# One core, two-layer trunk: the first V tiles take the last four U tiles from SBUF, gates are stored in pieces, one row of U per tile

## The chip, the core and the metric

The kernel runs on one core of one Trainium2 chip. The metric is the device time of one execution in microseconds. The median of three runs of the kernel before is 3313.8 us (3308.7 to 3314.72).

## The reference

Two layers. Layer 0 mixes with mLSTM heads and a short convolution, layer 1 with stick-breaking attention. After each mixer stands the same PEER block, which the change touches: every token picks 8 x 16 = 128 of 16384 experts by product keys, and each expert is one row of `expert_u` and one of `expert_v`.

```python
def peer_ffn(h, w_query, sub_keys1, sub_keys2, expert_u, expert_v):
    ...                                   # q, s1, s2, two top-k, softmax
    expert = e1 * PEER_NKEYS + e2
    def block(args):
        xt, et, gt = args
        act = jax.nn.gelu(jnp.einsum("td,thkd->thk", xt, expert_u[et]), approximate=False) * gt
        return jnp.einsum("thk,thkd->td", act, expert_v[et])
```

## The kernel before

All activations are float32; each matmul operand is split in a high and a low part, and three matmuls make one product. Weights come as a stream of 613 tiles of 128 x 1024 (`raw`, 512 KB, a ring of four, loaded by SyncE). ScalarE makes `w_hi` (L497), and `w_lo` is made by GpSimd (L434) or by VectorE (L1667).

The PEER block of a layer computes 384 of the 512 tokens densely, over all 16384 experts, and the last 128 tokens by fetching each token's own 128 rows of U and V ("fetched" tokens, one row of every token at a time, 512 KB).

The dense part is 128 U tiles (one per second key, numbered n), then 128 V tiles (numbered v). A U tile is 24 matmuls of 384 columns (L924 to L926), after which ScalarE takes gelu into `gel`, a ring of four slots (L679), and stores 192 KB of it to DRAM (`gel_dram`, L681). A V tile is 18 matmuls of 512 columns (L944), which sum the product of gelu and gate with V.

The gates come up during U tiles 27 to 116: VectorE builds one-hot planes for four tokens at a time (a quad, L1676 and L1680), TensorE multiplies them (L1176), and ScalarE and VectorE collect the result in `stage`. Twelve quads are a batch of 48 tokens; there are eight. ScalarE stores a batch of 3072 KB to `g_dram` in one DMA (L722); the eighth goes out at tile n = 117. The stage has 48 x 4 bytes x 128 keys = 24 KB in a row per partition.

At n = 121 (`FIRST_UNIT_AT`) ScalarE waits until all gates and the first eight gelus are in DRAM and loads two units. A unit is what four V tiles need: `gates` (768 KB, L730) and `gin`, the gelus (768 KB, L732). VectorE multiplies them (`product`, L1724), ScalarE rounds (`a_hi`, L740), VectorE subtracts (`a_lo`, L1732). This runs V_AHEAD = 5 tiles ahead of TensorE, so its first five stand in U tiles 123 to 127; unit 2 is loaded at n = 127. ScalarE loads the next unit when VectorE has finished the one before the last.

In each U tile from 27 on GpSimd fetches one row of U (L451) and VectorE takes its dot product with the token (`dot`, L1699); behind tile 117 there are two rows per tile. The ring `u_rows` has three slots. The rows left over, 17 of 128, follow one per V tile. GpSimd fetches rows of V (L459) once the last U tile is done, since their buffer lies over `h_lo`, and VectorE adds them up (L1711, L1714).

In U tiles up to 116 GpSimd makes `w_lo`; from 117 on VectorE does, two tiles ahead (`LOW_AHEAD`). Every engine's order is written out by hand. In a U tile ScalarE does `w_hi` of tile n + 3, the quads' copies, gelu, the store, and then what the tile number adds. In a V tile VectorE does `w_lo` of v + 2, `product` of v + 5, a dot if one is left, the row of V, and `a_lo` of v + 5. In layer 0 one of seven V tiles also has a dot product for the modulation (`ada_w`, 512 KB).

## Time and profile before

| | us |
|---|---|
| median of three runs | 3313.8 |
| profiled execution, device time | 3312.34 |
| its span | 3310.6 |
| TensorE busy | 3108.2 |
| VectorE busy | 2745.8 |

| transfer | KB each | count |
|---|---|---|
| raw (weight tile) | 512 | 613 |
| gel_dram store | 192 | 256 |
| g_dram store | 3072 | 16 |
| gates load, gin load | 768 | 64 each |

Of 317118 DMA packets all but 2366 are under 8 KB; the sixteen stores of gates have 128 rows of 24 KB each, 2048 in all. The profile's page gives busy time by engine, then the span in 40 slices, the queues, the chain that ended last, and the costliest groups. The timeline lists single instructions; in brackets stands how long the engine was idle ahead of one and what ended that.

### The profile page before, as it was taken

To read this page: it belongs to the slowest core of one execution; us is meant where nothing else is said; L and a number is where in the kernel's file an instruction comes from. 1 tells how busy PE (TensorE), PEld (TensorE's weight loads), DVE (VectorE), ACT (ScalarE), POOL (GpSimd) and SP (SyncE) were. 2 spreads that over 40 slices of the span, in tenths; PEclk is the share of its full clock that TensorE was granted. 3 is DMA by queue.
4 is the path that set the end of the run, shared out by engine and by line. 5 is a ranking of instruction groups with operands and counts; after the bars stand their busy time and mean duration, and the time that the engine had idled before them with its cause. 6 is when DMAs were issued, how large, how long until landed. Compare 5 with 4: busy or idle time off the path is not lost.

```text
span 3310.6 us, 44003 instructions
## 1 busy us (share of the span) xinstructions
PE 3108.2 (94%) x15340; PEld 2686.9 (81%) x15340; DVE 2745.8 (83%) x4632; ACT 1290.8 (39%) x1910; POOL 1532.8 (46%) x880
## 2 busy tenths in 40 slices
PE   4898999999997899999899998999999988999999
PEld 3776799999996677887777667899999976788887
DVE  6677898999996788887776658998999977878887
ACT  3233334444442233333344763344444432333332
POOL 3333346666664434344333003456666654556221
PEclk9899999999998999999999999999999998999999
DMA  5633246898889999999624013258898999999996
GB/s 220 204 121 110 75 129 202 291 319 300 311 307 339 369 367 354 359 367 354 249 77 153 1 51 118 96 174 271 305 317 308 314 325 359 366 366 358 366 354 234
DMA packets 317118, 849.16 MB, mean 256 GB/s; under 512 B 26144, under 2 KB 157232, under 8 KB 314752
## 3 DMA queue, kind: packets, MB, share of 16 engines
q1 hardware_dynamic: 90448, 329.82, 28.4%
q0 software_dynamic: 74000, 268.81, 22.6%
q10 hardware_dynamic: 152480, 248.02, 20.7%
q8 instruction: 117, 1.92, 0.2%
q14 instruction: 73, 0.60, 0.1%
HBM read 743.78 MB, written 102.76 MB: 256 GB/s over the span
## 4 chain that ended last, share of the span: by engine, by line
PE 45%; DVE 28%; DMA 14%; issue 8%; POOL 3%; ACT 1%; ACTq 0%; POOLq 0%; DVEq 0%; SPq 0%
PE banks L944 14%; DVE u_rows L1699 9%; PE gbank L944 7%; DVE plane L1680 6%; DMA u_rows<-u_dram,row_of 6%; DVE hot L1676 6%; DMA gin<-gel_dram 3%; PE banks L904 3%; PE banks L906 3%; PE banks L905 3%; DVE stage L1690 3%; DMA ada_w<-ada_dram 2%; PE banks L924 2%; PE banks L926 2%; PE banks L925 2%
## 5 line engine op out<-in xcount | busy, mean ns | idle before, releaser
L434 POOL TENSOR_TENSOR w_lo<-raw,w_hi 128x1024 fp32r<-128x1024 f32 x339 | 829.2, 2448 | 775.3 <-ACT w_hi L497 771.2
L497 ACT ACTIVATE w_hi<-raw 128x1024 fp32r<-128x1024 f32 x613 | 647.6, 1057 | 494.2 <-PE banks L944 229.2
L924 PE MATMUL banks<-h_hi,w_hi 128*128 128x384 f32 x2048 | 690.5, 337 | 31.2 <-DVE w_lo L1667 17.0
L925 PE MATMUL banks<-h_lo,w_hi 128*128 128x384 f32 x2048 | 688.3, 336 | 0.0
L926 PE MATMUL banks<-h_hi,w_lo 128*128 128x384 f32 x2048 | 688.0, 336 | 0.0
L459 POOL DMA_INDIRECT v_rows<-v_dram,row_of x256 | 421.6, 1647 | 532.0 <-DVE fetched L1714 518.4
L451 POOL DMA_INDIRECT u_rows<-u_dram,row_of x256 | 273.8, 1069 | 440.3 <-DVE z L1699 434.1
L1699 DVE CUSTOM_DVE_ANT_0 u_rows<-u_rows,h_rows 128x1024 f32<-128x1024 f32 x256 | 410.7, 1605 | 65.2 <-DMA u_rows<-u_dram,row_of 64.8
L924 PEld LDWEIGHTS banks<-h_hi,w_hi 128*128 128x128 f32 x2048 | 387.3, 189 | 33.0 <-DVE w_lo L1667 18.3
L925 PEld LDWEIGHTS banks<-h_lo,w_hi 128*128 128x128 f32 x2048 | 387.4, 189 | 0.0
L926 PEld LDWEIGHTS banks<-h_hi,w_lo 128*128 128x128 f32 x2048 | 387.0, 189 | 0.0
L1714 DVE SCALAR_TENSOR_TENSOR fetched<-v_rows,share,fetched 128x1024 f32<-128x1024 f32 x254 | 324.9, 1279 | 19.0 <-DMA v_rows<-v_dram,row_of 18.3
L1667 DVE TENSOR_TENSOR w_lo<-raw,w_hi 128x1024 fp32r<-128x1024 f32 x274 | 333.9, 1219 | 4.7 <-ACT w_hi L497 4.7
L740 ACT ACTIVATE a_hi<-gin 128x384 fp32r<-128x384 f32 x256 | 133.6, 522 | 490.9 <-DVE gin L1724 482.8
L944 PE MATMUL banks<-w_hi,a_hi 128*128 128x512 f32 x1024 | 321.9, 396 | 0.0
L944 PE MATMUL banks<-w_hi,a_lo 128*128 128x512 f32 x1024 | 319.8, 394 | 0.0
L944 PE MATMUL banks<-w_lo,a_hi 128*128 128x512 f32 x1024 | 318.8, 393 | 0.0
L904 PE MATMUL banks<-h_hi,w_hi 128*128 128x512 f32 x696 | 285.5, 410 | 2.2 <-DVE h_lo L1832 1.4
L906 PE MATMUL banks<-h_hi,w_lo 128*128 128x512 f32 x696 | 272.8, 392 | 0.0
L905 PE MATMUL banks<-h_lo,w_hi 128*128 128x512 f32 x696 | 272.5, 392 | 0.0
L679 ACT ACTIVATE gel<-banks 128x384 f32<-128x384 f32 x256 | 125.7, 491 | 356.1 <-PE banks L926 341.3
L1680 DVE TENSOR_TENSOR plane<-hot,banks 128x1024 fp32r<-128x1024 f32 x192 | 234.4, 1221 | 6.6
(316 smaller groups left out, 4852.2 us busy)
## 6 DMA issues: line engine op xcount, KB each, us to landing
raw<-stream_dram SPq DMA_DIRECT2D x613, 512.0 KB
gel_dram<-gel ACTq DMA_DIRECT2D x256, 192.0 KB
g_dram<-stage ACTq DMA_DIRECT2D x16, 3072.0 KB
gates<-g_dram ACTq DMA_DIRECT2D x64, 768.0 KB
gin<-gel_dram ACTq DMA_DIRECT2D x64, 768.0 KB
ada_w<-ada_dram ACTq DMA_DIRECT2D x50, 512.0 KB, 4.8
ada_out<-ada_dram ACTq DMA_DIRECT2D x18, 512.0 KB, 4.7
ada_first<-ada_dram SPq DMA_DIRECT2D x8, 1024.0 KB, 20.0
```

What stands on the lines that cost most here:

```text
L434: pool.tensor_tensor(w_lo[:, s, :], raw[:, s, :], w_hi[:, s, :].bitcast(F32), ALU.subtract).then_inc(split_lo, 1)
L459: pool.indirect_dma_start(v_rows[:, j % V_ROWS, :], None, (v0, v1)[layer], bass.IndirectOffsetOnAxis(ap=row_of[:, j:j + 1], axis=0)).then_ ...
L497: act.activation(w_hi[:, s, :], raw[:, s, :], ACT.Copy).then_inc(split_hi, 1)
L904: pe.matmul(out, wh, hi(k), start=(k == 0), stop=False)
L905: pe.matmul(out, wh, lo(k), start=False, stop=False)
L906: mm = pe.matmul(out, wl, hi(k), start=False, stop=(k == DC - 1))
L924: pe.matmul(out, wh, h_hi[:, k, 0:DENSE_T], start=(k == 0), stop=False)
L925: pe.matmul(out, wh, h_lo[:, k, 0:DENSE_T], start=False, stop=False)
L926: mm = pe.matmul(out, wl, h_hi[:, k, 0:DENSE_T], start=False, stop=(k == DC - 1))
L944: mm = pe.matmul(sums[c][half][:], a, w[:, half * SEQ:(half + 1) * SEQ], start=(v == 0 and a is ah and w is hi), stop=(v == NKEYS - 1 and ...
L1680: dve.tensor_tensor(plane[:, q % 2].rearrange("p t n e -> p n t e"), hot[:, q % 2, 1].bitcast(F32).unsqueeze(1).to_broadcast(full), parts[ ...
L1699: dve.tensor_tensor_reduce(row, row, h_rows[:], 1.0, 0.0, ALU.mult, ALU.add, z[:, j:j + 1]).then_inc(S("dotted"), 1)
```

## The change

- Unit 0 of V is now the last four U tiles. V on the host is rolled by four tiles, so V tile 0 is key 124. The gelus of n = 124 to 127 are not stored and not loaded: `product`, `a_hi` and `a_lo` of V tiles 0 to 3 work on `gel`. Unit 0 loads only gates.
- `V_AHEAD` is 3: the first three products stand in U tiles 125 to 127, the fourth in V tile 0. Unit 2 is loaded in V tile 1.
- A batch of gates is stored as four pieces of 32 keys (768 KB, rows of 6 KB), one per U tile for the first seven batches. The four pieces of the eighth batch all go at n = 117.
- One row of U per tile up to n = 127, so 101 rows in U tiles and 27 in V tiles (111 and 17 before). `u_rows` has four slots.

```diff
--- before.py
+++ after.py
@@ -24,7 +24,9 @@
 PH = 8
 TOPK = 16
 NKEYS = 128
-V_AHEAD = 5
+V_AHEAD = 3
+
+KEPT = 4
 A_RING = 8
 UNIT = 4
 
@@ -36,11 +38,12 @@
 DENSE_T = SEQ - FETCHED
 DENSE_C = DENSE_T // P
 PICKS = PH * TOPK
-U_ROWS, V_ROWS = 3, 4
+U_ROWS, V_ROWS = 4, 4
 QUADS = DENSE_T // QUAD
 QUAD_FROM = U_EARLY * DC + 12
 LOW_AHEAD = 2
 BATCH = 48
+PIECES = 4
 NBATCH = DENSE_T // BATCH
 BATCH_QUADS = BATCH // QUAD
 
@@ -62,8 +65,7 @@
 
     if n < ROWS_FROM:
         return range(0)
-    first = n - ROWS_FROM + max(n - U_GATED - 1, 0)
-    return range(first, min(PICKS, first + (2 if n > U_GATED else 1)))
+    return range(n - ROWS_FROM, n - ROWS_FROM + 1)
 
 
 U_DOTS = max(rows_of(n).stop for n in range(U_EARLY, NKEYS))
@@ -111,10 +113,10 @@
 
 
 COUNTS = {"scores": N_WQ, "sc": N_WQ, "ranked": N_WQ, "gate_arg": 1, "gate_exp": 1, "ex": 3, "ex_tp": 3,
-          "exT": 5, "hot": QUADS, "one": QUADS, "g_mm": QUADS, "g_hi": QUADS, "g_out": QUADS, "stored0": 16 * ((NBATCH + 1) // 2), "stored1": 16 * (NBATCH // 2), "picked": 2,
+          "exT": 5, "hot": QUADS, "one": QUADS, "g_mm": QUADS, "g_hi": QUADS, "g_out": QUADS, "stored0": 16 * PIECES * ((NBATCH + 1) // 2), "stored1": 16 * PIECES * (NBATCH // 2), "picked": 2,
           "h_rows": 1, "h_copied": 1, "v_row": 16 * PICKS // V_ROWS, "dotted": PICKS, "z_gel": 2,
           "added": PICKS, "acc": DENSE_C - 1, "y_rows": 2 * DENSE_C, "turned": DC,
-          "gel_stored": 16 * (NKEYS // 4), "unit": 16 * NKEYS // UNIT, "product": NKEYS, "a_hi": NKEYS,
+          "gel_stored": 16 * (NKEYS // 4 - 1), "unit0": 16 * NKEYS // UNIT - 16, "unit1": 16 * NKEYS // UNIT, "product": NKEYS, "a_hi": NKEYS,
           "acted": NKEYS}
 
 NORMS = ("n0", "f0", "n1", "f1")
@@ -677,6 +679,8 @@
                 act.wait_ge(tile_done, t + 1 + off)
                 wait(act, stored[s], past["gel_stored"] + 16 * (n // 4) + off * 4)
                 act.activation(gel[:, s, :], bank[t % 2][:, 0:DENSE_T], ACT.Gelu).then_inc(emptied_sem["a"], 1)
+                if n >= NKEYS - KEPT:
+                    return
                 act.wait_ge(emptied_sem["a"], emptied("a", t) + off)
                 act.dma_start(gel_dram[layer][ds(n + off, 1)].rearrange("a p t -> p (a t)"), gel[:, s, :]
                               ).then_inc(stored[s], 16)
@@ -712,53 +716,58 @@
                 b, o = q // BATCH_QUADS, QUAD * (q % BATCH_QUADS)
                 act.wait_ge(S("g_mm"), past["g_mm"] + q + 1)
                 if b >= 2 and o == 0:
-                    act.wait_ge(S(f"stored{b % 2}"), past[f"stored{b % 2}"] + 16 * (b // 2))
+                    act.wait_ge(S(f"stored{b % 2}"), past[f"stored{b % 2}"] + 16 * PIECES * (b // 2))
                 act.activation(stage[:, b % 2, :, o:o + QUAD], gbank[q % 2][:, :, 0].rearrange("p t e -> p e t"),
                                ACT.Copy).then_inc(S("g_hi"), 1)
 
-            def store_batch(b):
-
+            def store_piece(b, i):
+
+                own = slice(i * NKEYS // PIECES, (i + 1) * NKEYS // PIECES)
                 act.wait_ge(S("g_out"), past["g_out"] + BATCH_QUADS * (b + 1))
-                act.dma_start(g_dram[layer][b].rearrange("p e t -> p (e t)"),
-                              stage[:, b % 2, :, :].rearrange("p e t -> p (e t)")).then_inc(S(f"stored{b % 2}"), 16)
+                act.dma_start(g_dram[layer][b][:, own].rearrange("p e t -> p (e t)"),
+                              stage[:, b % 2, own, :].rearrange("p e t -> p (e t)")).then_inc(S(f"stored{b % 2}"), 16)
 
             def load_unit(u, off=0):
 
                 if not isinstance(off, int) or u >= 2:
                     act.wait_ge(S("acted"), past["acted"] + UNIT * (u - 1) + off * UNIT)
                 b = u % 2
+                own = ds((u * UNIT - KEPT) % NKEYS, UNIT)
                 act.dma_start(gates[:, b, :, :, :], g_dram[layer].rearrange("b p e t -> p b e t")[
-                    :, :, ds(u * UNIT + off * UNIT, UNIT), :]).then_inc(S(f"unit{b}"), 16)
-                act.dma_start(gin[:, b, :, :], gel_dram[layer].rearrange("e p t -> p e t")[
-                    :, ds(u * UNIT + off * UNIT, UNIT), :]).then_inc(S(f"unit{b}"), 16)
+                    :, :, own, :]).then_inc(S(f"unit{b}"), 16)
+                if u * UNIT >= KEPT:
+                    act.dma_start(gin[:, b, :, :], gel_dram[layer].rearrange("e p t -> p e t")[
+                        :, own, :]).then_inc(S(f"unit{b}"), 16)
 
 
             def a_high(n, off=0):
 
-                x = gin[:, n // UNIT % 2, n % UNIT, :]
+                x = gel[:, n % 4, :] if n < KEPT else gin[:, n // UNIT % 2, n % UNIT, :]
                 act.wait_ge(S("product"), past["product"] + n + 1 + off)
                 act.activation(a_hi[:, n % A_RING, :], x, ACT.Copy).then_inc(S("a_hi"), 1)
 
             batch_at = {quad_step(BATCH_QUADS * b + BATCH_QUADS - 1) // DC + 1: b for b in range(NBATCH)}
             for n in range(U_EARLY, NKEYS):
                 u_tile(n, quads=[q for q in range(QUADS) if quad_step(q) // DC == n])
-                if n in batch_at:
-                    store_batch(batch_at[n])
+                for i in range(PIECES):
+                    if n - i in batch_at and (i == 0 or batch_at[n - i] < NBATCH - 1):
+                        store_piece(batch_at[n - i], i)
+                if batch_at.get(n) == NBATCH - 1:
+                    for i in range(1, PIECES):
+                        store_piece(NBATCH - 1, i)
                 if n == FIRST_UNIT_AT:
                     for s in range(2):
-                        act.wait_ge(S(f"stored{s}"), past[f"stored{s}"] + 16 * ((NBATCH + 1 - s) // 2))
+                        act.wait_ge(S(f"stored{s}"), past[f"stored{s}"] + 16 * PIECES * ((NBATCH + 1 - s) // 2))
                     for s in range(4):
                         act.wait_ge(stored[s], past["gel_stored"] + 16 * (2 * UNIT // 4))
                     for u in range(2):
                         load_unit(u)
                 m = n - NKEYS + V_AHEAD
                 if m >= 0:
-                    if m and m % UNIT == 0:
-                        load_unit(m // UNIT + 1)
                     a_high(m)
 
             for s in range(4):
-                act.wait_ge(stored[s], past["gel_stored"] + 16 * (NKEYS // 4))
+                act.wait_ge(stored[s], past["gel_stored"] + 16 * (NKEYS // 4 - 1))
 
             def gelu_rows(n):
 
@@ -1719,8 +1728,11 @@
 
                 u, j = n // UNIT, n % UNIT
                 if j == 0:
-                    dve.wait_ge(S(f"unit{u % 2}"), past["unit"] + 32 * (u // 2 + 1) + off * (16 // UNIT))
+                    dve.wait_ge(S(f"unit{u % 2}"), past[f"unit{u % 2}"] + 32 * (u // 2 + 1) - (0 if u % 2 else 16))
                 x = gin[:, u % 2, j, :]
+                if n < KEPT:
+                    dve.wait_ge(emptied_sem["a"], emptied("a", DENSE[layer] + NKEYS - KEPT + n))
+                    x = gel[:, n % 4, :]
                 dve.tensor_tensor(x.rearrange("p (b t) -> p b t", b=NBATCH),
                                   x.rearrange("p (b t) -> p b t", b=NBATCH),
                                   gates[:, u % 2, :, j, :], ALU.mult).then_inc(S("product"), 1)
@@ -1729,7 +1741,8 @@
 
                 hi, lo = a_hi[:, n % A_RING, :], a_lo[:, n % A_RING, :]
                 dve.wait_ge(S("a_hi"), past["a_hi"] + n + 1 + off)
-                dve.tensor_tensor(lo, gin[:, n // UNIT % 2, n % UNIT, :], hi.bitcast(F32), ALU.subtract
+                x = gel[:, n % 4, :] if n < KEPT else gin[:, n // UNIT % 2, n % UNIT, :]
+                dve.tensor_tensor(lo, x, hi.bitcast(F32), ALU.subtract
                                   ).then_inc(S("acted"), 1)
 
             q = 0
@@ -1863,7 +1876,7 @@
 
 
         ut = u.reshape(P, NKEYS, DC, P).transpose(1, 3, 2, 0).reshape(NKEYS, P, D)
-        vt = v.reshape(P, NKEYS, D).transpose(1, 0, 2)
+        vt = np.roll(v.reshape(P, NKEYS, D).transpose(1, 0, 2), KEPT, 0)
         return [ut, vt]
 
     def col(v, n=D):
```

ScalarE, layer 0, from U tile 117 on: the gelu and its store, then the last batch of gates. Before:

```order
L497 ACTIVATE w_hi<-raw 128x1024
L679 ACTIVATE gel<-banks 128x384
L681 DMA gel_dram<-gel 128x384
L722 DMA g_dram<-stage 128x6144
L497 ACTIVATE w_hi<-raw 128x1024
```

In the change, the same place:

```order
L499 ACTIVATE w_hi<-raw 128x1024
L681 ACTIVATE gel<-banks 128x384
L685 DMA gel_dram<-gel 128x384
L727 DMA g_dram<-stage 128x1536 x4
L499 ACTIVATE w_hi<-raw 128x1024
```

The one store has become four in a row; nothing stands between them.

ScalarE, layer 0, U tile 121 and the start of 122: the first units. Before:

```order
L679 ACTIVATE gel<-banks 128x384
L681 DMA gel_dram<-gel 128x384
L730 DMA gates<-g_dram 128x8x192
L732 DMA gin<-gel_dram 128x4x384
L730 DMA gates<-g_dram 128x8x192
L732 DMA gin<-gel_dram 128x4x384
L497 ACTIVATE w_hi<-raw 128x1024
```

In the change:

```order
L681 ACTIVATE gel<-banks 128x384
L685 DMA gel_dram<-gel 128x384
L736 DMA gates<-g_dram 128x8x192 x2
L739 DMA gin<-gel_dram 128x4x384
L499 ACTIVATE w_hi<-raw 128x1024
```

Four loads ahead of the next `w_hi` have become three; the load of unit 0's gelus is gone.

VectorE, layer 0, a U tile near the end that has a product (`z` is the sum that a dot leaves). Before, tile 123:

```order
L1667 TENSOR_TENSOR w_lo<-raw,w_hi 128x1024
L1699 ISA u_rows,z<-u_rows,h_rows 128x1024
L1699 ISA z 128x1
L1699 ISA u_rows,z<-u_rows,h_rows 128x1024
L1699 ISA z 128x1
L1724 TENSOR_TENSOR gin<-gin,gates 128x384
L1732 TENSOR_TENSOR a_lo<-gin,a_hi 128x384
```

In the change, tile 125:

```order
L1676 TENSOR_TENSOR w_lo<-raw,w_hi 128x1024
L1708 ISA u_rows,z<-u_rows,h_rows 128x1024
L1708 ISA z 128x1
L1736 TENSOR_TENSOR gel<-gel,gates 128x384
L1745 TENSOR_TENSOR a_lo<-gel,a_hi 128x384
```

One dot less per tile, and the product is on `gel`.

## Rows read from the trace of the kernel before

**Rows 1.** The page: busy us, share of the span, instructions.
```profile
PE 3108.2 (94%) x15340; PEld 2686.9 (81%) x15340; DVE 2745.8 (83%) x4632; ACT 1290.8 (39%) x1910; POOL 1532.8 (46%) x880
```

**Rows 2.** ScalarE's timeline, layer 0: start, duration, engine, line, operation [idle, ended by].
```profile
1002.38 0.49 ACT L679 ACTIVATE gel<-banks 128x384 f32<-128x384 f32 x1 [2.14 <-PE banks L926]
...
1003.28 0.53 ACTq L722 DMA_DIRECT2D g_dram<-stage  x1
...
1018.57 1.06 ACT L497 ACTIVATE w_hi<-raw 128x1024 fp32r<-128x1024 f32 x1 [7.38 <-DMA raw<-stream_dram]
...
1029.84 0.49 ACT L679 ACTIVATE gel<-banks 128x384 f32<-128x384 f32 x1 [7.26 <-PE banks L926]
...
1033.27 9.70 ACTq L732 DMA_DIRECT2D gin<-gel_dram  x1
1043.07 1.06 ACT L497 ACTIVATE w_hi<-raw 128x1024 fp32r<-128x1024 f32 x1 [12.74 <-issue]
...
1045.96 0.47 ACT L679 ACTIVATE gel<-banks 128x384 f32<-128x384 f32 x1
...
1070.72 0.47 ACT L679 ACTIVATE gel<-banks 128x384 f32<-128x384 f32 x1
```

**Rows 3.** The same of layer 1.
```profile
2687.35 0.49 ACT L679 ACTIVATE gel<-banks 128x384 f32<-128x384 f32 x1 [2.13 <-PE banks L926]
...
2713.19 0.49 ACT L679 ACTIVATE gel<-banks 128x384 f32<-128x384 f32 x1 [6.76 <-PE banks L926]
...
2716.63 10.84 ACTq L732 DMA_DIRECT2D gin<-gel_dram  x1
...
2730.46 0.47 ACT L679 ACTIVATE gel<-banks 128x384 f32<-128x384 f32 x1
...
2754.94 0.47 ACT L679 ACTIVATE gel<-banks 128x384 f32<-128x384 f32 x1
```

**Rows 4.** TensorE's timeline: V tile 0 and V tile 3 of layer 0.
```profile
1071.45 1.19 PE L944 MATMUL gbank<-w_hi,a_hi 128*128 128x512 f32 x2 [6.96 <-ACT gel L679]
...
1087.96 0.73 PE L944 MATMUL gbank<-w_hi,a_hi 128*128 128x512 f32 x2 [2.03 <-DVE w_lo L1667]
```

**Rows 5.** TensorE's timeline: V tile 0 of layer 1.
```profile
2755.66 1.19 PE L944 MATMUL gbank<-w_hi,a_hi 128*128 128x512 f32 x2 [6.56 <-ACT gel L679]
```

**Rows 6.** The chain that ended last, layer 1's V: start, us, what.
```profile
2857.17 2.72 PE banks L944 x12
...
3101.97 2.72 PE banks L944 x12
```

**Rows 7.** Windows: us, busy by engine (instructions), granted TensorE clock, DMA share, GB/s.
```profile
1002.00:1071.00 69.00, 46.62 (x242) 45.37 (x241) 39.09 (x57) 16.66 (x25) 25.69 (x21) 0.86 0.95 351
1085.00:1176.00 91.00, 77.34 (x295) 59.82 (x294) 77.77 (x107) 23.86 (x33) 40.96 (x31) 0.91 0.97 368
1180.00:1637.00 457.00, 445.78 (x1943) 366.90 (x1943) 371.34 (x459) 164.79 (x215) 198.99 (x109) 0.99 0.93 353
```

**Rows 8.** VectorE's timeline, layer 0: the first row of V, and the 18th.
```profile
1085.55 0.75 DVE L1711 TENSOR_SCALAR fetched<-v_rows,share 128x1024 f32<-128x1024 f32 x1 [6.84 <-DMA v_rows<-v_dram,row_of]
...
1175.78 1.28 DVE L1714 SCALAR_TENSOR_TENSOR fetched<-v_rows,share,fetched 128x1024 f32<-128x1024 f32 x1
```

**Rows 9.** VectorE's timeline, layer 1: the first row of V, and the 17th.
```profile
2769.34 0.75 DVE L1711 TENSOR_SCALAR fetched<-v_rows,share 128x1024 f32<-128x1024 f32 x1 [5.43 <-DMA v_rows<-v_dram,row_of]
...
2851.27 1.28 DVE L1714 SCALAR_TENSOR_TENSOR fetched<-v_rows,share,fetched 128x1024 f32<-128x1024 f32 x1
```

**Rows 10.** GpSimd's timeline, layer 0: the first row of V is asked for.
```profile
1075.27 1.32 POOL L459 DMA_INDIRECT v_rows<-v_dram,row_of  x1 [0.30 <-issue]
```

**Rows 11.** VectorE's waits, U tiles with quads of layer 0: total us, times, longest.
```profile
DVE u_rows L1699 <- DMA u_rows<-u_dram,row_of: 5.2, 4, 2.1
```

**Rows 12.** The same of layer 1.
```profile
DVE u_rows L1699 <- DMA u_rows<-u_dram,row_of: 3.9, 4, 1.8
```

**Rows 13.** All waits of the kernel: VectorE for the gelus of a unit.
```profile
DVE gin L1724 <- DMA gin<-gel_dram: 80.8, 22, 7.5
```

## The prediction

> **What bounds the kernel now.** I read the busy times first: TensorE is busy 94% of the span [rows 1], so only its idle stretches can be won. The change touches the PEER blocks, so the next view is ScalarE's timeline around U tile 117, because gelus there mark the end of each U tile. The reader should take the differences of the gelu times. A tile costs 4.08 us when nothing holds TensorE up: in layer 1's V, 60 tiles take 3101.97 - 2857.17 = 244.8 us [rows 6], and a U tile has as many columns (24 x 384 = 18 x 512).
>
> From the gelu of tile 117 to V tile 0 there are ten tiles, 40.8 us, and 0.7 us from the last gelu to V (1070.72 to 1071.45). Layer 0 takes 1071.45 - 1002.38 = 69.1 us [rows 2, 4], layer 1 2755.66 - 2687.35 = 68.3 us [rows 3, 5]. So 27.6 and 26.8 us are lost, 54.4 in all. They fall in three parts:
>
> - **The burst**, tiles 118 to 121: 27.5 - 16.3 = 11.1 us and 25.8 - 16.3 = 9.5 us. The 3072 KB store goes at 1003.28; ScalarE then waits 7.38 us for a weight tile [rows 2].
> - **The issue jam**, tiles 122 and 123: 16.1 - 8.2 = 8.0 us and 17.3 - 8.2 = 9.1 us. The fourth load of the first units holds ScalarE for 9.70 and 10.84 us [rows 2, 3], so ScalarE starts its next `w_hi` only after 12.74 us, and TensorE waits for gelu.
> - **The double rows**, tiles 124 to 127: 24.8 - 16.3 = 8.4 us and 24.5 - 16.3 = 8.2 us. VectorE has two dots, a product and `w_lo` in a tile, and its rows come late; gelu stands behind `a_hi`, which waits for VectorE. This ends with TensorE idle for 6.96 and 6.56 us ahead of V [rows 4, 5].
>
> Under all three lies the DMA: in these 69 us it is 95% busy at 351 GB/s, and 97% at 368 GB/s in the V tiles with dots [rows 7]. That is the second bound, and it caps what the first can give back.
>
> **The change part by part.**
>
> *The tail of U.* I price it by bytes. Before, 69 us x 351 GB/s = 24.2 MB. Ten rows of U leave (10 x 0.52 = 5.2 MB), the gelus of unit 0 (0.8 MB) and four gelu stores (0.8 MB). 17.4 MB are left, which take 47.3 us at the 368 GB/s of the next stretch. TensorE alone would need 41.5 us. I take 47.3, since that is the later of the two: gain 69.1 - 47.3 = 21.8 us and 68.3 - 47.3 = 21.0 us, together **-42.8**. The ends are 0 and -54.4.
>
> Why the three losses should go: the store's rows are 6 KB instead of 24 KB, beside weight tiles in rows of 4 KB, so in the same queue turns it takes less of the time. The three loads that remain are the number that before went out in 0.95 + 0.90 us and a little, ahead of the long one: unit 0's and 1's gates and one gelu load have as many rows (2560) as the first three before. A tile has one dot. New is that ScalarE will reach n = 121 while the store is still running: it comes there 16.3 us after the store was issued, and 3.1 MB beside the rest need about 20 us (3.1 of every 7 MB moved at 351 GB/s). It then waits some 4 to 5 us. Behind that wait stand `w_hi` of tile 125 and gelu of 122. TensorE has `w_lo` up to tile 123 or 124 and needs gelu 122 only for tile 124, some 8 us later. So I cost that wait at nothing; if the store takes 8 us longer than that, each further us counts.
>
> The Trainium skill, "DMA: Bandwidth & Descriptors", section "Queues, rings and completion order", says that each DMA engine takes turns between queues, one packet at a time. By that rule a store in 24 KB rows beside two streams in 4 KB rows would have 24 of 32 KB, and in 6 KB rows 6 of 14.
>
> A rule that speaks against the pieces: a stretch in which no transfer is larger than 768 KB moves 368 GB/s [rows 7], no less than the one that holds the 3072 KB store. The same page, section "Bandwidth", wants 1 MiB or more per transfer and gives 341 GB/s at 1 MB against 425 GB/s at 16 MB. As an estimate from that page, 3.1 MB at 341 instead of 400 GB/s would be 1.3 us more per batch, some 21 us for sixteen if nothing hid it, and 3303 us in the end. The trace does not agree with that price.
>
> *The ten dots in V.* They move from the tail into V tiles 17 to 26. There VectorE's rows of V stand 5.31 us apart in layer 0 (1175.78 - 1085.55, 17 tiles) [rows 8] and 5.12 us in layer 1 (81.9 us, 16 tiles) [rows 9]. Without dots a V tile costs 457 / 108 = 4.23 us in layer 0 (1943 matmuls, 18 a tile) [rows 7] and 4.08 in layer 1 [rows 6]. So 10 x 1.08 + 10 x 1.04 = **+21.2**. The ends: nothing, if four slots hide it, and 2 x 10 x 1.43 = 28.6 us, which is 0.52 MB at 368 GB/s for each row.
>
> *The start of V.* Before, V tile 3 began 16.5 us after V tile 0 instead of 12.2 [rows 4]: 2.03 us of waiting for `w_lo`, which stands behind the first row of V, and the rest slow matmuls after 6.96 us of idleness (the granted clock of the tail is 0.86 [rows 7]). The row was asked for 3.8 us after V began, because GpSimd still had a late row of U ahead of it, and landed 10.3 us later [rows 8, 10]. In the change GpSimd has nothing late, so the row comes about when tile 3 needs it. I take back 4 of the 4.3 us in layer 0 and 3 in layer 1, where the first row came 13.7 us after V began instead of 14.1 [rows 5, 9]: **-7** (ends 0 and -9).
>
> *The earlier stores and the fourth slot.* VectorE waited for rows of U 5.2 and 3.9 us there, at stores [rows 11, 12]. A fourth slot gives each row one tile more, and pieces spread the store. VectorE and TensorE take turns as the bound there, so I count a third: **-3** (ends 0 and -9.1). The 42 further DMA instructions cost ScalarE about half a us each [rows 2] and ScalarE is 39% busy: nothing.
>
> *V_AHEAD 3.* `w_lo` is only two tiles ahead, and `a_lo` of v + 3 is ready before `w_lo` of v + 3. So the shorter lead is hidden behind `w_lo`: 0. The load of a unit and its product stay four tiles apart.
>
> **The sum**: 3312.3 - 42.8 + 21.2 - 7 - 3 = 3280.7 us against the profiled execution. That lies 1.5 us below the median of 3313.8, so I forecast **3282 us**.
>
> **The rivals.**
>
> *The bytes rule it all.* From tile 117 to V tile 27 the DMA is the bound before and after, in V without dots too (353 GB/s [rows 7]). Then moving rows gives nothing, and only the 1.6 MB that are gone count: 4.4 us per layer. With the -3 above that is 3302 us. For it: 95 to 97% busy. Against it: layer 1's V runs at exactly TensorE's pace [rows 6].
>
> *One stall stays.* The jam stays with three loads (its 17.1 us), or the burst, since the last four pieces go at once (20.6 us). Then the tail gives 37.3 or 33.8 us instead of 42.8: 3288 or 3291, or up to 3299 if the time at the DMA comes on top. Against the jam: the first three loads went out quickly.
>
> *Both stay*, so the split does not do what it says: only 16.7 us of the tail come back, 3308 us.
>
> *Slower: the lead of three is too short.* VectorE waits for units 22 times, 80.8 us in all, at most 7.5 us [rows 13], and TensorE hardly feels it. If a late unit reached TensorE now, all of it would cost: 3282 + 81 = 3363 us; half of it gives 3322. It decides from where VectorE is late by more than two tiles, 8.2 us. Against: the longest wait is below that, and the two-tile bound was there before.
>
> **How the numbers follow.** The forecast has 0.50 (3264 to 3290), the bytes 0.17, one stall 0.12, both 0.09, the lead 0.12. The range of 3264 to 3308 leaves out the lead and the low end beyond: if the tail reached 41.5 us and VectorE hid half of the dots, it would be 3282 - 11.6 - 10.6 = 3260. A measurement can tell 0.2% from no change, 6.6 us, so the bound is 3307. Faster: 0.50 + 0.17 + 0.12 = 0.79; the same: 0.09; slower: 0.12.
>
> **What the profile would show.** If the steps are right, from gelu 117 to V tile 0 there are about 47 us with no wait of TensorE above 3 us, no load issue on ScalarE above 2 us, and a wait of under 8 us ahead of the unit loads. Rows of V stand 5.1 to 5.3 us apart for 27 tiles. VectorE's waits for rows of U in the quads' stretch are near zero. The forecast is wrong if a load issue still takes 9 us, if ScalarE still waits 7 us for a weight tile behind the last store, if V's dots cost clearly more than 1.1 us each, or if TensorE waits for `a_lo` anywhere in V.

## The result, and the profile after

The change gives 3288.3 us (median of 8 runs, 3281.5 to 3301.5) beside 3312.2 us for the kernel before (8 runs, 3302.9 to 3323.4). The ratio is 0.9933, 95% interval 0.9910 to 0.9956, so 15 to 30 us faster. The profiled execution was the slowest of the eight: 3301.5 us, span 3299.8.

ScalarE in layer 0 from gelu 117 on, to be held against [rows 2] (start, duration, engine, line, operation, in brackets the idle time before and what ended it):

```profile
998.89 0.49 ACT L681 ACTIVATE gel<-banks 128x384 f32<-128x384 f32 x1 [2.13 <-PE banks L935]
...
999.79 2.91 ACTq L727 DMA_DIRECT2D g_dram<-stage  x4
...
1015.53 0.49 ACT L681 ACTIVATE gel<-banks 128x384 f32<-128x384 f32 x1 [1.98 <-PE banks L935]
1016.05 0.34 ACTq L685 DMA_DIRECT2D gel_dram<-gel  x1
1024.84 3.90 ACTq L736 DMA_DIRECT2D gates<-g_dram  x2
1028.77 3.21 ACTq L739 DMA_DIRECT2D gin<-gel_dram  x1
1032.08 1.06 ACT L499 ACTIVATE w_hi<-raw 128x1024 fp32r<-128x1024 f32 x1 [16.06 <-DMA gel_dram<-gel]
1033.04 0.47 ACT L681 ACTIVATE gel<-banks 128x384 f32<-128x384 f32 x1
...
1034.97 0.47 ACT L681 ACTIVATE gel<-banks 128x384 f32<-128x384 f32 x1
...
1052.60 0.49 ACT L681 ACTIVATE gel<-banks 128x384 f32<-128x384 f32 x1 [2.31 <-PE banks L935]
```

Gelu 121 comes 16.64 us after gelu 117, which is TensorE's own 4.16 us a tile; before it took 27.5. Then ScalarE does no work for 16.06 us: first it waits for the last pieces of the gates (8.5 us, till 1024.84), then come its own three load instructions (3.90 + 3.21 us). The row names a gelu store as what ended the wait. But ScalarE waits there for all gates and for the first eight gelus, which had long landed, and the last 6 KB packet of the gates ends at 1024.27 in this trace. Gelus 122 and 123 come 19.4 us after 121 (16.1 before), and the last four take 17.6 us (24.8 before). TensorE, to be held against [rows 4, 5]:

```profile
1033.66 0.66 PE L933 MATMUL banks<-h_hi,w_hi 128*128 128x384 f32 x1 [9.85 <-ACT gel L681]
...
1053.35 0.70 PE L953 MATMUL gbank<-w_hi,a_hi 128*128 128x512 f32 x2 [0.78 <-ACT gel L681]
...
1065.69 0.61 PE L953 MATMUL gbank<-w_hi,a_hi 128*128 128x512 f32 x2
...
2742.00 0.70 PE L953 MATMUL gbank<-w_hi,a_hi 128*128 128x512 f32 x2 [0.78 <-ACT gel L681]
```

One long wait is left, 9.85 us for gelu 122. V starts after 0.78 us instead of 6.96 and 6.56, and V tile 3 follows 12.3 us after tile 0 instead of 16.5. The windows, to be held against [rows 7] (us, busy time and instructions by engine, granted TensorE clock, DMA share, GB/s):

```profile
999.00:1053.00 54.00, 43.72 (x240) 43.11 (x238) 27.61 (x38) 15.96 (x24) 17.48 (x13) 0.91 0.94 350
1064.00:1170.00 106.00, 91.92 (x365) 71.50 (x364) 90.74 (x123) 28.11 (x38) 50.21 (x38) 0.94 0.99 377
1184.00:1628.00 444.00, 428.47 (x1851) 352.20 (x1849) 362.78 (x449) 156.92 (x208) 187.35 (x104) 0.98 0.93 350
1005.00:1045.00 40.00, 30.16 (x163) 29.86 (x162) 15.96 (x22) 10.48 (x15) 11.22 (x8) 0.87 1.02 401
1039.00:1059.00 20.00, 19.22 (x104) 17.96 (x103) 12.48 (x21) 8.76 (x14) 7.97 (x7) 1.00 0.76 261
```

The DMA is full, at 401 GB/s, while ScalarE stands still, and has slack (261 GB/s, 76%) in the 20 us around V tile 0. In the V tiles with dots it is fuller than before (377 GB/s, 99%).

VectorE's rows of V, to be held against [rows 8, 9], and its waits in the whole kernel (total us, times, longest):

```profile
1058.27 0.75 DVE L1720 TENSOR_SCALAR fetched<-v_rows,share 128x1024 f32<-128x1024 f32 x1 [1.26 <-DMA v_rows<-v_dram,row_of]
...
1205.40 1.28 DVE L1723 SCALAR_TENSOR_TENSOR fetched<-v_rows,share,fetched 128x1024 f32<-128x1024 f32 x1
...
2748.21 0.76 DVE L1720 TENSOR_SCALAR fetched<-v_rows,share 128x1024 f32<-128x1024 f32 x1 [2.54 <-DMA v_rows<-v_dram,row_of]
...
2882.35 1.28 DVE L1723 SCALAR_TENSOR_TENSOR fetched<-v_rows,share,fetched 128x1024 f32<-128x1024 f32 x1
```

```profile
DVE gin L1736 <- DMA gin<-gel_dram: 70.6, 22, 7.6
DVE fetched L1723 <- DMA v_rows<-v_dram,row_of: 35.3, 23, 3.2
...
DVE u_rows L1708 <- DMA u_rows<-u_dram,row_of: 14.7, 8, 2.3
```

Of each pair of rows of V the second is the 27th, so they stand 5.66 us apart in layer 0 and 5.16 in layer 1 (5.31 and 5.12 before). VectorE does not wait for rows of U in the stretch with the quads any more (5.2 and 3.9 us before [rows 11, 12]).

**The ledger.** Three marks read from the timelines divide each kernel's time: gelu 117, the first matmul of V, and ScalarE's last copy into `y_rows` (1628.21 and 3290.10 us in the change). "Tail" is the first stretch, "V" the second. The four columns ahead of them divide the tail (the step from gelu 127 to V, 0.7 us in all, is not shown).

| us, layer 0 / layer 1 | gelu 117 to 121 | 121 to 123 | 123 to 127 | tail | V | both |
|---|---|---|---|---|---|---|
| before | 27.5 / 25.8 | 16.1 / 17.3 | 24.8 / 24.5 | 69.1 / 68.3 | 566.0 / 544.9 | 635.1 / 613.2 |
| the change | 16.6 / 16.6 | 19.4 / 19.0 | 17.6 / 18.4 | 54.5 / 54.8 | 574.9 / 548.1 | 629.3 / 602.9 |
| e1 loads at tile 123 | 16.6 / 16.6 | 13.2 / 14.1 | 20.7 / 19.9 | 51.3 / 51.4 | 566.3 / 546.0 | 617.6 / 597.4 |
| e2 pieces only | 21.5 / 19.3 | 18.1 / 17.3 | 25.9 / 26.3 | 66.2 / 63.6 | 565.9 / 545.2 | 632.1 / 608.8 |
| e3 one row only | 20.7 / 19.0 | 16.0 / 17.0 | 17.6 / 17.4 | 55.1 / 54.2 | 587.3 / 551.5 | 642.4 / 605.7 |
| e4 kept tiles only | 27.4 / 26.5 | 13.1 / 13.6 | 27.2 / 27.1 | 68.3 / 68.0 | 562.8 / 541.1 | 631.2 / 609.1 |
| e5 spread store | 16.6 / 16.6 | 8.3 / 8.3 | 26.2 / 25.7 | 52.0 / 51.4 | 566.0 / 548.6 | 617.9 / 600.1 |
| e6 and spread loads | 16.6 / 16.6 | 8.3 / 8.3 | 23.2 / 23.9 | 48.9 / 49.7 | 568.7 / 553.8 | 617.6 / 603.5 |
| e7 no dots in V | 16.6 / 16.6 | 19.2 / 17.9 | 17.6 / 18.4 | 54.2 / 53.7 | 546.9 / 522.5 | 601.1 / 576.2 |
| e8 dots, no fetch | 16.6 / 16.6 | 19.0 / 18.5 | 17.9 / 18.3 | 54.2 / 54.2 | 548.0 / 526.6 | 602.3 / 580.8 |
| e9 whole batches | 20.2 / 19.3 | 15.4 / 15.2 | 17.6 / 17.9 | 54.0 / 53.1 | 568.1 / 552.0 | 622.0 / 605.1 |
| e10 two rows | 16.6 / 16.6 | 23.8 / 23.5 | 19.3 / 19.4 | 60.5 / 60.3 | 560.9 / 539.6 | 621.4 / 599.9 |
| e11 before, lead 3 | 27.3 / 25.9 | 15.7 / 14.1 | 23.5 / 28.1 | 67.1 / 68.8 | 570.3 / 545.5 | 637.4 / 614.3 |
| e12 three slots | 16.7 / 16.6 | 18.6 / 18.0 | 17.9 / 18.2 | 53.9 / 53.6 | 572.6 / 550.6 | 626.5 / 604.1 |

From before to the change the tail gives back 14.6 + 13.5 = 28.1 us and V takes 8.9 + 3.2 = 12.1. The U tiles ahead of gelu 117 give 3.3 + 0.2 = 3.5. That is 19.5 us. The profiled execution then lost 9.2 us between the layers (503.3 us from the last `y_rows` of layer 0 to the first gelu of layer 1, 494.1 before), where no line was changed. There the granted clock differs. Windows, before and then the change:

```profile
1800.00:1860.00 60.00, 57.24 (x224) 34.14 (x223) 35.44 (x75) 40.17 (x93) 3.35 (x2) 0.86 0.08 28
```

```profile
1800.00:1860.00 60.00, 57.91 (x179) 30.35 (x180) 30.46 (x69) 37.40 (x88) 0.00 (x0) 0.69 0.00 1
1810.00:1830.00 20.00, 20.00 (x50) 10.84 (x50) 10.36 (x26) 11.35 (x28) 0.00 (x0) 0.50 0.00 1
```

For 20 us it is 0.50, the 1.2 GHz level, in the change's execution. Over the ten kernels from e1 to e6 and e9 to e12 the same stretch takes 495.0 to 499.1 us, so 494.1 and 503.3 are two ends of what executions do. TensorE stood idle for 2.8 us between 1790 and 1820 in both executions; behind that the clock was 0.66 for 20 us before, and 0.50 and then 0.84 for 40 us more in the change's. The ledger leaves this stretch out; the medians hold it. One execution of e11, of 7837.7 us, was disturbed and is left out of everything below.

### The profile page after: what moved, and what is told of

Same layout as the page of the kernel before. It is cut to its first block, busy times and chain, and to the rows that moved or that the text cites. A ratio compares the mean times of both kernels' runs of the same rounds, so it can differ in the third digit from the quotient of the medians.

```text
span 3299.8 us, 44043 instructions
## 1 busy us (share of the span) xinstructions
PE 3114.6 (94%) x15340; PEld 2685.8 (81%) x15340; DVE 2749.2 (83%) x4632; ACT 1292.4 (39%) x1910; POOL 1532.8 (46%) x880
## 4 chain that ended last, share of the span: by engine, by line
PE 44%; DVE 32%; DMA 12%; issue 8%; POOL 3%; ACTq 1%; ACT 1%; POOLq 0%; DVEq 0%; SPq 0%
PE banks L953 10%; DVE u_rows L1708 9%; DVE plane L1689 7%; DVE hot L1685 6%; PE gbank L953 5%; DMA gin<-gel_dram 4%; DMA v_rows<-v_dram,row_of 4%; DMA ada_w<-ada_dram 3%; PE banks L913 3%; PE banks L915 3%; PE banks L914 3%; PE banks L933 3%; DVE stage L1699 3%; PE banks L935 3%; PE banks L934 3%
## 5 line engine op out<-in xcount | busy, mean ns | idle before, releaser
L933 PE MATMUL banks<-h_hi,w_hi 128*128 128x384 f32 x2048 | 688.6, 336 | 19.3 <-ACT gel L681 19.3
L461 POOL DMA_INDIRECT v_rows<-v_dram,row_of x256 | 414.6, 1620 | 510.3 <-DVE fetched L1723 487.4
L1708 DVE CUSTOM_DVE_ANT_0 u_rows<-u_rows,h_rows 128x1024 f32<-128x1024 f32 x256 | 417.2, 1630 | 14.7 <-DMA u_rows<-u_dram,row_of 14.7
L1676 DVE TENSOR_TENSOR w_lo<-raw,w_hi 128x1024 fp32r<-128x1024 f32 x274 | 333.7, 1218 | 26.2 <-ACT w_hi L499 26.2
```

Of the source, the lines that this page charges most:

```text
L461: pool.indirect_dma_start(v_rows[:, j % V_ROWS, :], None, (v0, v1)[layer], bass.IndirectOffsetOnAxis(ap=row_of[:, j:j + 1], axis=0)).then_ ...
L933: pe.matmul(out, wh, h_hi[:, k, 0:DENSE_T], start=(k == 0), stop=False)
L1708: dve.tensor_tensor_reduce(row, row, h_rows[:], 1.0, 0.0, ALU.mult, ALU.add, z[:, j:j + 1]).then_inc(S("dotted"), 1)
```

## The experiments

Ratios are to runs of the kernel before on the same chip, and need not equal the quotient of two medians given here. V is read with care, since there is one trace of each kernel: in the change, e1, e5, e6, e9 and e12, whose V tiles hold the same work, it took 566.0 to 574.9 us in layer 0 and 546.0 to 553.8 in layer 1, and the change's own trace is the highest of layer 0.

**Each part alone**

e2 stores the gates of the kernel before in four pieces a batch, at the tiles where the change does.

```diff
-                if n in batch_at:
-                    store_batch(batch_at[n])
+                for i in range(PIECES):
+                    if n - i in batch_at and (i == 0 or batch_at[n - i] < NBATCH - 1):
+                        store_piece(batch_at[n - i], i)
...
```

> The kernel before, with the gates stored in four pieces a batch and nothing else. Stall theory: tiles 118 to 121 fall from 27.5 and 25.8 us to 17 or 18, ScalarE then waits for the store as in the changed kernel and tiles 122 and 123 grow from 16.1 and 17.3 to about 19 or more, tiles 124 to 127 stay near 24.6. The sum is 12 to 16 us less, with 3 for the earlier stores: 3297 us. Byte theory: no byte is gone, so all of it comes back by V tile 20: 3312 us.

Measured: 3302.3 us, ratio 0.9967 (0.9948 to 0.9986). The burst of tiles 118 to 121 loses 4.8 and 2.7 us instead of 10.8 and 9.2. The six tiles behind it take 3.1 and 1.8 us more. The time lies between the stall theory's 3297 and the byte theory's 3312.

e3 takes one row of U per tile in the kernel before.

```diff
-    first = n - ROWS_FROM + max(n - U_GATED - 1, 0)
-    return range(first, min(PICKS, first + (2 if n > U_GATED else 1)))
+    return range(n - ROWS_FROM, n - ROWS_FROM + 1)
```

> The kernel before, with one row of U per tile to the end of U (27 rows left for V instead of 17) and nothing else. Stall theory: tiles 124 to 127 fall from 24.8 and 24.5 us to 17 to 20, the burst and the jam stay (27.5 and 25.8, 16.1 and 17.3 us), the start of V is 3 us quicker in each layer, and the ten more dots cost 21 us: 3306 to 3312 us. Byte theory: the rows only change their place: 3312 us. If a dot in V cost 1.4 us of DMA time or more, it would be 3318.

Measured: 3310.4 us, ratio 0.9992 (0.9972 to 1.0012), no change. Its tail, 55.1 and 54.2 us, is that of the whole change, though its gates go out in one store: the double rows had a part in the burst's loss too. V takes 21.3 and 6.6 us of it back. Over both layers the tail is shorter by 28.1 us, and V longer by 27.9.

e4 keeps the last four U tiles on chip, with the lead of three, and has neither pieces nor single rows nor the fourth slot.

```diff
-U_ROWS, V_ROWS = 4, 4
+U_ROWS, V_ROWS = 3, 4
...
-PIECES = 4
+PIECES = 1
...
-    return range(n - ROWS_FROM, n - ROWS_FROM + 1)
+    first = n - ROWS_FROM + max(n - U_GATED - 1, 0)
+    return range(first, min(PICKS, first + (2 if n > U_GATED else 1)))
```

> The changed kernel with whole batches stored, two rows of U per tile and three slots: what is left is that V begins with the last four U tiles, whose gelu stays on chip, with V_AHEAD 3. Stall theory: the burst stays (27 and 26 us for tiles 118 to 121), tiles 122 and 123 lose less than 16.1 and 17.3 us because a load is gone (10 to 14), tiles 124 to 127 fall to about 20, because the products start two tiles later: 3296 us. Byte theory: 1.57 MB less per layer, 4.4 us each: 3303 us.

Measured: 3306.0 us, ratio 0.9973 (0.9954 to 0.9993). From gelu 117 to the end it gains 3.9 and 4.1 us a layer. The 1.6 MB that are gone are worth 4.4 us in the prediction's price by bytes, and about that comes out. The stall theory's 20 us for tiles 124 to 127 did not come (27.2 and 27.1).

The product of the three ratios is 0.9932, and the change has 0.9933. So close an agreement is luck, since each of the ratios is known to 0.2% only; it shows that no large term beyond the three is needed.

**The jam at tile 121**

e1 moves the first loads of units two tiles later in the change, so that the gates have time to land.

```diff
-FIRST_UNIT_AT = U_GATED + 4
+FIRST_UNIT_AT = U_GATED + 6
```

> The changed kernel, with ScalarE's wait for the stored gates and the first unit loads at U tile 123 instead of 121. Stall theory (the loss that is left in the tail, 17.5 + 1.9 us over tiles 122 and 123 where 8.2 are needed, is ScalarE standing 8.2 us for the store and 7 us in issuing loads, with w_hi and gelu queued behind): two tiles later the store has landed, the wait is under 1 us, the 7 us of issue fit in TensorE's slack of about 8 us. From gelu 117 to V tile 0 it takes 43 to 47 us instead of 54.5 and 54.8, and the kernel 3268 us. Byte theory (the tail is bound by the DMA at about 350 GB/s): the stretch stays at 53 to 55 us, or what it gives comes back in the first ten V tiles; 3286 to 3290 us.

Measured: 3284.0 us, ratio 0.9920 (0.9894 to 0.9946). ScalarE, layer 0:

```profile
1018.48 0.49 ACT L681 ACTIVATE gel<-banks 128x384 f32<-128x384 f32 x1 [2.00 <-PE banks L935]
...
1028.75 0.49 ACT L681 ACTIVATE gel<-banks 128x384 f32<-128x384 f32 x1 [7.94 <-DMA gel_dram<-gel]
...
1032.81 2.86 ACTq L736 DMA_DIRECT2D gates<-g_dram  x2
1035.70 4.87 ACTq L739 DMA_DIRECT2D gin<-gel_dram  x1
1040.67 1.06 ACT L499 ACTIVATE w_hi<-raw 128x1024 fp32r<-128x1024 f32 x1 [8.49 <-issue]
```

The wait for the gates is gone, and the 9.85 us of TensorE with it (the longest wait left for a gelu is 2.73 us in layer 0 and 3.6 in layer 1). But a second blocker comes out. Gelu 122 waits 7.94 us until the 192 KB of gelu 118 have left its slot: that store was issued behind the four pieces on the same queue. The Trainium skill, "DMA: Bandwidth & Descriptors", section "Queues, rings and completion order", says that each DMA engine consumes a queue's descriptors in ring order; this row agrees: the store was issued at 1007.23, and ScalarE was released at 1028.75, 21.5 us later. The three load instructions still take 7.7 us. The tail (51.3 us) and the time miss the stall theory's 43 to 47 and 3268 us; the time is nearer to the byte theory's 3286.

e5 spreads the last batch's pieces over tiles 117 to 120, beside e1's edit.

```diff
-                    if n - i in batch_at and (i == 0 or batch_at[n - i] < NBATCH - 1):
+                    if n - i in batch_at:
                         store_piece(batch_at[n - i], i)
-                if batch_at.get(n) == NBATCH - 1:
-                    for i in range(1, PIECES):
-                        store_piece(NBATCH - 1, i)
```

> As the run with late loads (first units at tile 123), and the last batch's four pieces one per tile at 117 to 120. There, gelu 122 waited 7.9 us for the store of gelu 118, which stood in ScalarE's DMA queue behind all four pieces (25 to 26 us). Queue theory (transfers of one queue go in order, so a burst of 3 MB also holds up the small stores that the ring of four gelu slots needs): the store of gelu 118 is now behind two pieces only, gelu 122 comes 4.16 us after 121, and the stall is what is left at the unit loads. Tiles 122 and 123 take 8.3 to 10 us instead of 13.2 and 14.1, and from gelu 117 to V tile 0 it takes 46 to 49 us. Byte theory: the 3 MB are through at the same time whatever their order, the loads wait at 123 until then, and the stretch stays at 51 us.

Measured: 3289.1 us, ratio 0.9922 (0.9892 to 0.9952). ScalarE, layer 0:

```profile
1027.87 0.49 ACT L681 ACTIVATE gel<-banks 128x384 f32<-128x384 f32 x1 [2.13 <-PE banks L932]
...
1036.36 1.63 ACTq L736 DMA_DIRECT2D gates<-g_dram  x2
1038.02 3.27 ACTq L739 DMA_DIRECT2D gin<-gel_dram  x1
1041.38 1.06 ACT L499 ACTIVATE w_hi<-raw 128x1024 fp32r<-128x1024 f32 x1 [13.03 <-DMA gel_dram<-gel]
```

Now the gelus up to 123 stand at 4.16 us, and the whole loss sits one step later: ScalarE can go on only at 1036.36 us, 33 us after the first piece was issued. The queue theory had the step from 121 to 123 (8.3 us), and the byte theory the tail, which is what it was in e1.

e6 keeps that and splits the loads: unit 0's gates at tile 123, unit 1's gates at 125, its gelus at 127.

```diff
-                    for u in range(2):
-                        load_unit(u)
+                    load_unit(0)
+                if n == FIRST_UNIT_AT + 2:
+                    load_unit(1, parts=(0,))
+                if n == FIRST_UNIT_AT + 4:
+                    load_unit(1, parts=(1,))
```

> As the run with late loads and pieces one per tile, and the first unit loads split: gates of unit 0 at tile 123, gates of unit 1 at 125, gelus of unit 1 at 127. Queue theory: three loads in a row took ScalarE 7 us to issue, because the third finds the queue full; apart, each takes 1 to 3 us and hides behind TensorE. From gelu 117 to V tile 0 it takes 43 to 46 us. Byte theory: 50 us or more, or the unit 1 that comes later makes VectorE wait at V tile 1 and gives it back in V.

Measured: 3287.4 us, ratio 0.9923 (0.9896 to 0.9950). Loads and the first row of V, layer 0:

```profile
1034.81 0.39 ACTq L737 DMA_DIRECT2D gates<-g_dram  x1
1037.05 0.38 ACTq L737 DMA_DIRECT2D gates<-g_dram  x1
1047.91 0.43 ACTq L740 DMA_DIRECT2D gin<-gel_dram  x1
```

```profile
1059.31 0.75 DVE L1721 TENSOR_SCALAR fetched<-v_rows,share 128x1024 f32<-128x1024 f32 x1 [5.90 <-DMA v_rows<-v_dram,row_of]
```

A load apart from the others issues in 0.4 us, here and in layer 1, so the 7 us came from what was queued just before and not from the instruction itself. The tail falls to 48.9 and 49.7 us. The gates still land late (1034.81 us), and TensorE waits 3.9 us for a gelu. V then waits 5.90 us for its first row (1.26 in the change), which shares the DMA with the load from tile 127, and is 2.7 and 5.2 us longer than in e5, where the tail gave 3.0 and 1.8. From gelu 117 to the end e1, e5 and e6 are equal within 0.3 us in layer 0 and 6 us in layer 1. The DMA in the same 40 us of e1, and then of e5:

```profile
1005.00:1045.00 40.00, 34.66 (x186) 34.07 (x185) 18.02 (x24) 12.33 (x17) 12.80 (x9) 0.94 1.03 403
```

```profile
1005.00:1045.00 40.00, 33.19 (x186) 32.90 (x185) 18.69 (x25) 11.55 (x16) 12.77 (x9) 0.92 1.03 399
```

It is as full as in the change (401 GB/s). Three orders of the same bytes end in the same time within the intervals, which is what a full DMA behind the jam would give. The three are some 0.1% better than the change, and the intervals of 0.2 to 0.3% each do not tell that from nothing.

**What a dot in V costs**

e7 leaves out the 27 dots of V tiles, and the 24 fetches for them that are issued in V.

```diff
-                if U_DOTS + U_ROWS - 1 + j < PICKS:
-                    u_fetch(layer, U_DOTS + U_ROWS - 1 + j)
...
-                    dot(U_DOTS + v)
+                    j = U_DOTS + v
+                    dve.memset(z[:, j:j + 1], 0.0).then_inc(S("dotted"), 1)
```

> The changed kernel without the rows of U of V: their fetches but for three and their 27 dots are left out (the sums of those 27 rows are zero). This is the price of 27 dots in V. Prediction's step: 27 x 1.08 and 27 x 1.04, so V falls from 574.9 and 548.1 us by 29 and 28, but not below 522 us, TensorE's own time, plus what the modulation's loads cost in layer 0.

Measured: 3232.7 us, ratio 0.9742 (0.9707 to 0.9777). V is shorter by 27.9 and 25.6 us than in the change's trace, 1.03 and 0.95 a dot (in layer 0 19 us, 0.7 a dot, against the shortest V with 27 dots).

e8 leaves out the same fetches, and the dots work on what lies in the ring.

```diff
-                dve.wait_ge(S(f"u_row{layer}_{j % U_ROWS}"), 16 * (j // U_ROWS + 1))
+                if j < U_DOTS + U_ROWS - 1:
+                    dve.wait_ge(S(f"u_row{layer}_{j % U_ROWS}"), 16 * (j // U_ROWS + 1))
```

> The changed kernel with all 27 dots in V, but 24 of the fetches left out; those dots run on rows that are already there (their results are wrong). It tells VectorE's time from the DMA's. VectorE theory (a V tile with a dot takes VectorE 4.42 us, more than TensorE's 4.08): V is only a little shorter than in the changed kernel, its tiles with dots 4.4 us. DMA theory (a row costs 0.52 MB in a full stretch, and rows of V land late): V is nearly as short as without the dots, its tiles with dots 4.4 us at most and without waits for rows of V. Both say 4.42 as the floor; the difference of the two runs to it tells the shares: 0.34 x 27 = 9 us is VectorE's, the rest the DMA's.

Measured: 3246.8 us, ratio 0.9807 (0.9772 to 0.9841). V is shorter by 26.8 and 21.5 us. By these traces VectorE's work has 1.1 and 4.1 of those 27.9 and 25.6 us, and the fetched rows have the rest. That is VectorE's least share. In e7's layer 0 VectorE waits 17.4 us for the modulation's loads between 1054 and 1180 us, in e8 0.2, which can hide part of the difference. The medians of e7 and e8 are 14.1 us apart (four runs each, intervals that just overlap), a quarter of the 55.6 us from e7 to the change, where the traces' V gives 5.2. And in layer 1 of e8 VectorE works without a gap in V tiles with a dot, and its rows of V stand 4.42 us apart (5.16 in the change, 4.08 for TensorE alone), as expected:

```profile
2732.05 1.28 DVE L1722 SCALAR_TENSOR_TENSOR fetched<-v_rows,share,fetched 128x1024 f32<-128x1024 f32 x1
...
2736.47 1.28 DVE L1722 SCALAR_TENSOR_TENSOR fetched<-v_rows,share,fetched 128x1024 f32<-128x1024 f32 x1
```

So most of the price of a dot in V, some three quarters by the medians, is the DMA's.

**One part taken out of the change**

e9 has whole batches.

```diff
-PIECES = 4
+PIECES = 1
```

> The change, but each batch of gates is one store of 3072 KB again (rows of 24 KB) instead of four. Theory A (the pieces are what removed the burst's loss): gelus of tiles 118 to 121 stand some 5 us apart again, so these four take 20 to 27 us instead of 16.64, ScalarE waits for a weight tile of U behind the store, and from gelu 117 to V tile 0 it is 58 to 63 us instead of 54.5; the time rises by 8 to 16 us over the change, to some 3297 to 3305 us. Rival B (the one row a tile alone keeps the tiles at pace, and the pieces only moved the time): the four tiles stay under 18 us, the tail within 1.5 us of 54.5 and the time within 4 us of the change's 3288.

Measured: 3293.3 us, ratio 0.9935 (0.9912 to 0.9957). Neither expectation held in full. The burst loses 3.6 and 2.6 us again, and the jam gives as much back. ScalarE, layer 0:

```profile
1001.47 0.51 ACTq L727 DMA_DIRECT2D g_dram<-stage  x1
...
1014.37 1.06 ACT L499 ACTIVATE w_hi<-raw 128x1024 fp32r<-128x1024 f32 x1 [4.99 <-DMA raw<-stream_dram]
...
1020.78 0.47 ACT L681 ACTIVATE gel<-banks 128x384 f32<-128x384 f32 x1
...
1021.87 5.53 ACTq L736 DMA_DIRECT2D gates<-g_dram  x2
1027.42 5.38 ACTq L739 DMA_DIRECT2D gin<-gel_dram  x1
1032.91 1.06 ACT L499 ACTIVATE w_hi<-raw 128x1024 fp32r<-128x1024 f32 x1 [11.66 <-issue]
```

The whole store in 24 KB rows has landed within 20.4 us, and ScalarE, which is late itself, does not wait for it; four pieces in 6 KB rows took 25.1 us (999.79 to 1024.84). With the whole store ScalarE waits 4.99 and then 4.00 us for weight tiles, with the pieces 0.63 us at most. So the pieces let the weight tiles through and land later, and burst and jam trade places.

e10 fetches two rows of U per tile behind tile 117 again; its edit is e3's, the other way round.

```diff
-    return range(n - ROWS_FROM, n - ROWS_FROM + 1)
+    first = n - ROWS_FROM + max(n - U_GATED - 1, 0)
+    return range(first, min(PICKS, first + (2 if n > U_GATED else 1)))
```

> The change, but with two rows of U per tile behind tile 117 again (111 rows in U tiles, 17 in V). Theory A (the DMA is full, so a row costs 0.5 MB at 370 to 400 GB/s, 1.3 to 1.4 us, wherever it is fetched in the tail, and 1.0 us in V): from gelu 117 to V tile 0 it is 64 to 69 us instead of 54.5, V is 9 to 12 us shorter, and the sum per layer is 1 to 5 us worse than the change's. Rival B (with pieces and kept tiles the double rows cost nothing of their own): the tail stays under 60 us, V gets 10 us shorter, and the time falls to some 3275 us.

Measured: 3288.6 us, ratio 0.9936 (0.9916 to 0.9955), the change's own time. Its tail is 60.5 and 60.3 us, less than theory A had, and V is 13.9 and 8.5 us shorter. So the ten rows back in the tail cost 6.0 and 5.5 us there. Against the other kernels with 27 dots (e1, e5, e9, e12) V is 5.1 to 11.6 us shorter in layer 0 and 6.4 to 12.4 in layer 1, so it gives back about as much or more. Its windows from some 20 us after gelu 117 on, and from 40 us on, to be held against the change's last window above, and the 20 us around its own V tile 0 (1058.15 us):

```profile
1018.00:1038.00 20.00, 9.58 (x43) 8.97 (x42) 10.77 (x16) 2.29 (x3) 7.11 (x6) 0.79 1.04 409
1038.00:1058.00 20.00, 17.13 (x94) 16.81 (x92) 15.19 (x24) 7.27 (x12) 11.56 (x8) 0.95 0.96 345
1048.00:1068.00 20.00, 16.98 (x85) 14.99 (x84) 14.30 (x25) 6.86 (x11) 10.51 (x9) 1.00 0.85 274
```

From 40 us after gelu 117 on the change leaves a quarter of the DMA idle (76%); the double rows fill that time (96%), and around their own V tile 0 the DMA is at 85%. So part of the rows that the change took out of the tail had stood where the DMA now has room.

e11 is the kernel before with the products three tiles ahead.

```diff
-V_AHEAD = 5
+V_AHEAD = 3
```

> The kernel before, with the products of V three tiles ahead instead of five and nothing else. Theory A (the shorter lead is hidden behind the weight tiles' low parts, which are only two tiles ahead): V from tile 0 to the last row of y within 3 us of 566.0 and 544.9 us per layer, no wait of TensorE for the activations' low part above 1 us, the time within 0.2% of the kernel before. Rival B (a late unit now reaches TensorE): VectorE's waits for units, at most 7.5 us, come through, V grows by 10 to 80 us per layer.

Measured: 3316.0 us, ratio 1.0009 (0.9984 to 1.0034). TensorE has no wait for `a_lo` or `a_hi` in this trace or in the change's. V is 4.3 us longer in layer 0, where theory A allowed 3, and 0.6 in layer 1. e4 and e10, with the same lead and number of dots, have V shorter than before, so the lead is hardly what made it longer.

e12 has three slots for rows of U.

```diff
-U_ROWS, V_ROWS = 4, 4
+U_ROWS, V_ROWS = 3, 4
```

> The change, but the ring for rows of U has three slots again instead of four. Theory A (the fourth slot is what freed the stretch with the gates from waits for rows): VectorE's waits for rows of U rise from 14.7 us in all to 40 to 60 us, and the time by 2 to 6 us over the change. Rival B (the pieces did that, the slot nothing): the waits stay under 25 us and the time within 2 us of the change's.

Measured: 3294.3 us, ratio 0.9955 (0.9935 to 0.9975); held against the change's ratio, with both intervals, this leaves the slot's worth open between a loss of 3 us and a gain of 17. VectorE's waits for rows of U are 24.4 us in all, which is the rival's figure; the time is nearer to theory A's. The U tiles up to gelu 117 of layer 0 take 553.6 us here, 553.7 in e9, 553.6 in the change, 556.9 before. So pieces without the slot, or the slot without pieces, bring the 3 us there.

## Why the prediction came out right, and where it did not

The forecast was 3282 us with 3264 to 3308, and 3288.3 was measured. The total holds, with a gain of 23.9 us by the medians where 31.8 were forecast, but the case that it stood on, all three losses of the tail gone, is not the one that came. What came is the rival "one stall stays", the jam, which was priced at 3288. That this is the measured figure is luck: the rival had 37.3 us for the tail, or 25.7 us and 3299 with the time at the DMA on top, and the tail gave 28.1.

**Tail of U: -42.8 predicted, -28.1 measured.** This term was mis-sized by 14.7 us. Held against 4.16 us a tile, the pace of U tiles that nothing holds up (the prediction took V's 4.08), two of its three losses went as said: the burst from 10.8 and 9.2 us to nothing, the double rows from 8.1 and 7.8 us to 1.0 and 1.8. The jam grew, from 7.8 and 9.0 us to 11.1 and 10.7. Three steps failed in it. The store was put at about 20 us and took 25.1: its price came from the mean rate of the tail, and e9 shows that the pieces land later than the whole. The three loads were put below 2 us because their like had gone out in 0.95 + 0.90 us; they took 7.1 and 7.0. Those first three went out when nothing had to be waited for; here the gelu stores issued behind the pieces are still in the queue (e1 shows how late they land). That this made the difference is argued, not shown; e6 shows only that apart the loads take 0.4 us each. And the wait was costed at nothing under a cover of 8 us. The cover was smaller: of ScalarE's 16.06 us TensorE stood for 9.85, so 6.2 were covered, and the same 6.2 come out of e5 (13.03 and 6.8) and e6 (10.11 and 3.9). By it the store's wait alone would have cost TensorE some 2.6 us and the loads alone some 1.4, which is an estimate from these rows; in a row they cost 9.85.

**The bytes beneath it.** I priced the tail at 17.4 MB by 368 GB/s, 47.3 us. It moved 54 us x 350 GB/s = 18.9 MB. Most of the 1.5 MB more are fetched rows: their queue moved 10.14 MB in the tail before and 6.29 MB in the change's, 3.9 MB less where 5.2 had been taken off. e6, with the least of the jam left, has 48.9 and 49.7 us, close to that price, and gives it back in V. Of the jam's 11 us a layer, removing it in three ways brought 3 to 4 us of the total (0.9920 to 0.9923 against 0.9933). With intervals of 0.2 to 0.3% each that is not told from zero, nor from the 6 us that the change lacks to 3282; the single traces of e1, e5 and e6 are 11 to 17 us better from gelu 117 to the end, half or more of that in layer 0's V. The rival "the bytes rule it all" (3302) fits what lies under the jam best. As a total it was too dear, since it gave nothing to the removed burst, and e2 is 11 us better than before with all bytes in place.

**The ten dots in V: +21.2.** The pair e10 and the change has 13.9 + 8.5 = 22.4 us, e3 and before 27.9. With e1, e5, e9 and e12 in the change's place e10's V is 11.8 to 22.6 us shorter, so the size is right and its closeness is partly luck. The reason was half of it. I read it as VectorE and TensorE taking turns, with the bytes as an outer bound, and e8 shows that most of it is fetched rows. **The start of V: -7.** Its signs are there: 0.78 us of waiting, 12.3 us to tile 3, VectorE 1.26 us early for the row. Together the two terms were +14.2, and V took +12.1 in the change's trace, though only +1.4 in e1's, whose V tiles hold the same work. The spacing of 5.1 to 5.3 us for 27 tiles held in layer 1 (5.16) and not in layer 0 (5.66).

**One row a tile**, on which both the tail's and the dots' term rest, brings nothing that can be measured: e3 and e10 say so from both sides. The rows that would have told it were there before: a row costs 0.52 MB in the tail and 0.52 MB in V, and the DMA was at 95 to 97% in both.

**Earlier stores, fourth slot: -3.** 3.5 us measured ahead of gelu 117, nearly all in layer 0. **Lead of three: 0.** e11 bears it out within its interval; the rival that made it slower (3322 or 3363) found no wait of TensorE, and VectorE's longest wait for a unit is 7.6 us (7.5 before [rows 13]).

**The sum.** 3280.7 was predicted against the profiled execution, which came to 3301.5: 14.7 us from the tail, -2.1 from V, -0.5 from U, 9.2 from the clock between the layers, and 0.5 less in what is left. Set against the medians, 3312.2 to 3288.3, the gain is 23.9 us, and the ledger without that stretch has 19.5.

**The rule on 1 MiB.** The Trainium skill, "DMA: Bandwidth & Descriptors", section "Bandwidth", wants 1 MiB or more per transfer. As an estimate from its figures the pieces were to cost some 21 us in all, and the runs do not show that price. In the same 40 us the change's 768 KB stores moved 401 GB/s and the 3072 KB store of the kernel before 367. But the change differs from it in more than that; e9 differs from the change in the pieces alone. First the kernel before, then e9:

```profile
1005.00:1045.00 40.00, 25.06 (x130) 24.45 (x129) 18.19 (x26) 6.47 (x10) 13.73 (x11) 0.83 0.97 367
```

```profile
1005.00:1045.00 40.00, 31.30 (x166) 30.69 (x165) 16.61 (x22) 10.02 (x14) 11.65 (x9) 0.87 1.02 404
```

So the size of the stores costs nothing here (401 and 404 GB/s). What raised the rate from 367 is not settled: e2, with the pieces alone, has 410 in the same 40 us.

**What stays open.** Which of the parts the gain needs is not settled. Taken out one by one, pieces, single rows and slot each leave a time that the measurement does not tell from the change's, while pieces alone and kept tiles alone are each faster than before. The kept tiles were not taken out alone. Nor was it shown what makes V differ between like kernels, by 9 us in layer 0 and 8 in layer 1, so no difference of that size in one trace's V proves anything.

## What to carry to other kernels

When every stage around a stall keeps the DMA at 95% or more, price an edit by the bytes that it removes, and treat work that is moved from one such stage to the next as moved, not saved; look instead for a stretch in which the DMA has slack. A wait that is "covered" must be added to all that the same engine does next, its DMA instructions too, before it is held against the cover. A small store whose buffer is needed soon can be held up by a burst of megabytes ahead of it on its queue; here e5 removed that stall, and the time did not fall, since the DMA was full.

## What the runs showed of the hardware that I had not expected

- A DMA instruction's own time depends on what was queued just before it. One load of 768 KB issues in 0.38 to 0.43 us with the loads apart (e6); the same three in a row take 4.9 us (e5), 7.1 (the change), 7.7 (e1), 10.9 (e9) and 14.2 (e10).
- 192 KB issued behind 3 MB on ScalarE's queue held its buffer for 21.5 us (e1).
- The same 3 MB landed in under 20.4 us as 24 KB rows (e9) and in 25.1 us as 6 KB rows (the change), beside like traffic, though in 22.3 us in e10, beside more fetched rows.
- Mixed traffic of transfers of 192 to 768 KB held 399 to 411 GB/s over 40 us (e5, the change, e1, e10), and 404 with a 3072 KB store among them (e9).
- Two executions with nothing changed in the attention stage differ there by 9 us, one of them with 20 us at a granted clock of 0.50.
